# The shared expert's four up blocks, moved from behind the expert sweep into it

## The reference, cut to what matters

```python
def swiglu(x, w1, w3, w2):
    return (jax.nn.silu(x @ w1) * (x @ w3)) @ w2

def moe_ffn(xs, ...):                       # xs: 512 tokens, 64 experts, 6 of them per token
    ...
    yg = lax.map(expert_block, (xg, blk_e)).reshape(P, D) * slot_w[:, None]
    routed = jax.ops.segment_sum(yg, slot_tok, num_segments=T + 1)[:T]
    return routed + swiglu(xs, sh_w1, sh_w3, sh_w2)
```

## Time and profile before

| | us |
|---|---|
| median of 3 runs | 2140.44 (2139.7 to 2141.09) |
| the profiled execution | 2133.77 |
| its span, first to last instruction | 2131.8 |
| PE busy | 1854.0 (87%) |
| DVE busy | 859.0 (40%) |
| ACT busy | 461.1 (22%) |
| POOL busy | 373.6 (18%) |
| transfers, over the span | 625.10 MB, 293 GB/s |

### The profile page before, as it was taken

One profiled execution on the slowest core, in us unless ns is written; L12 is line 12 of the kernel. 1 busy time (PEld: TensorE's weight loads), 2 busy tenths in 40 slices (PEclk: granted clock), 3 DMA queues, 4 the chain that ended last, 5 costly groups with the idle time before them and its releaser, 6 DMA issues.

```text
span 2131.8 us, 30544 instructions
## 1 busy us (share of the span) xinstructions
PE 1854.0 (87%) x9472; PEld 966.6 (45%) x9473; DVE 859.0 (40%) x1527; ACT 461.1 (22%) x823; POOL 373.6 (18%) x563
## 2 busy tenths in 40 slices
PE   5989999885999888788998899876889899989996
PEld 3455555333544444444444443344444444444543
DVE  1546666556322222222115499566222221212226
ACT  4134444212101011111110565220111111101112
POOL 0010000001111111111105288002111111111113
PEclk9999999996999999999999999887999999999997
DMA  9488010347999999999997202256999999999955
GB/s 405 176 340 330 1 40 20 139 173 304 357 420 393 402 400 394 401 404 396 383 382 262 123 1 119 79 227 269 399 406 402 399 387 408 402 400 396 398 182 211
DMA packets 95680, 625.10 MB, mean 293 GB/s; under 512 B 16128, under 2 KB 16256, under 8 KB 57472
## 3 DMA queue, kind: packets, MB, share of 16 engines
q1 hardware_dynamic: 44640, 499.70, 58.3%
q0 software_dynamic: 26112, 79.72, 10.3%
q10 hardware_dynamic: 24864, 44.84, 5.8%
HBM read 563.38 MB, written 76.28 MB: 300 GB/s over the span
## 4 chain that ended last, share of the span: by engine, by line
PE 57%; DMA 19%; DVE 10%; issue 5%; POOL 5%; ACT 3%; SPq 0%; POOLq 0%; DVEq 0%; ACTq 0%
DMA ring<-in 18%; PE PS L1064 12%; PE PS L1058 9%; PE PS L1071 6%; PE PS L1096 4%; PE PS L1085 4%; PE PS L1286 3%; PE PS L1049 3%; PE PS L986 3%; POOL work L581 3%; POOL work L613 3%; PE PS L1040 2%; PE PS L949 2%; PE PS L1004 2%; PE PS L1014 2%
## 5 line engine op out<-in xcount | busy, mean ns | idle before, releaser
L1064 PE MATMUL PS<-ring,work 128*64 128x256 f32 x3360 | 419.6, 406 | 112.8 <-issue 110.2
L1064 PEld LDWEIGHTS PS<-ring,work 128*64 128x64 f32 x3360 | 248.0, 146 | 260.5 <-issue 165.6
L1457 DVE TENSOR_TENSOR work<-work,PS 64x256 f32<-64x256 f32 x105 | 44.4, 423 | 521.9 <-ACT work L666 520.0
L1071 PE MATMUL PS<-ring,work 128*64 128x512 f32 x840 | 203.3, 605 | 1.0 <-DVE work L1469 1.0
L1058 PE MATMUL PS<-ring,work 128*128 128x512 f32 x400 | 184.3, 615 | 19.9 <-issue 8.6
L533 POOL COPY col_i<-idx 128x1 int32 (+1 forms) x128 | 23.4, 182 | 793.2 <-PE PS L1096 785.8
L1463 DVE COPY work<-PS 128x1024 f32<-128x1024 f32 x128 | 156.7, 1225 | 13.6 <-PE PS L1096 9.7
L539 POOL DMA_INDIRECT work<-h_rows,col_i x128 | 124.9, 976 | 165.2 <-issue 165.2
L666 ACT ACTIVATE work<-PS 64x256 f32<-64x256 f32 x105 | 39.5, 376 | 519.1 <-PE PS L1064 516.7
L1096 PE MATMUL PS<-cst,work 128*128 128x128 f32 x1040 | 142.4, 281 | 9.9 <-DMA work<-h_rows,col_i 9.9
L1096 PEld LDWEIGHTS PS<-cst,work 128*128 128x128 f32 x1040 | 115.0, 142 | 62.9 <-issue 52.8
(11 more groups left out here) (247 smaller groups left out, 2176.9 us busy)
## 6 DMA issues: line engine op xcount, KB each, us to landing
ring<-in SPq DMA_DIRECT2D x156, 2048.0 KB, 8.6
ring<-in SPq DMA_DIRECT2D x132, 1024.0 KB, 11.0
y_rows<-sq POOLq DMA_DIRECT2D x2, 14336.0 KB, 58.0
y_rows<-work ACTq DMA_DIRECT2D x210, 128.0 KB
ring<-in SPq DMA_DIRECT2D x3, 4096.0 KB, 15.4
y_rows<-work ACTq DMA_DIRECT2D x46, 256.0 KB
ring<-in SPq DMA_DIRECT2D x2, 3072.0 KB, 16.8
work<-in SPq DMA_DIRECT2D x2, 2048.0 KB, 17.4
```

The source lines that it names most:

```text
L1064: last = mm(bank(6)[64 * q:64 * q + 64, 0:F], lhs(c)[:, 0:64], w13(s)[:, q, c, :], start=(c == 0), stop=(c == DC - 1), tile_position=(0, 6 ...
L1071: last = mm(bank(4)[64 * q:64 * q + 64, :], actT[par][:, kk, 0:64], w2(s)[:, kk, q * 512:(q + 1) * 512], start=(kk == 0), stop=(kk == 1), ...
```

## The change

- SP loads the shared up half (2 MB) into `acc` ahead of the sweep, right behind the fourth expert's weights and ahead of `refill_up(4)`. The load behind the sweep, with its wait, is gone. The down half stays where it was.
- The loops over experts 3 to 62 on TensorE, ACT and DVE are each cut into four loops of 4, 4, 4 and 3 rounds (`PARTS`).
- TensorE runs one shared block behind each of the four: behind experts 18, 34, 50 and 62, that is w1 and w3 for the first half of the features, then for the second half. The third waits for the first silu, the fourth for the first product.
- ACT does the first shared silu and DVE the first shared product behind their second loops. The second silu stays where it was (behind the extra unit); the second product moves ahead of the first combination.
- TensorE behind the sweep: expert 63, the extra unit, then at once the shared down.

```diff
+        shared_w13 = acc.rearrange("p t d -> p (t d)").rearrange("p (a c f) -> p a c f", a=2, c=DC)
+        PARTS = ((0, 4), (4, 8), (8, 12), (12, (E - 4) // 4))
@@ load_moe
+                sp.dma_start(acc.rearrange("p t d -> p (t d)"), sh_w[i][:, 0:UP]).then_inc(sh_in, 16)
                 refill_up(4, slot_of(4))
...
-                sp.wait_ge(m["up_ps"], E - 3)
-                sp.dma_start(slot_ap(SHARED)[:, 0:UP], sh_w[i][:, 0:UP]).then_inc(sh_in, 16)
                 refill_down(E - 1, slot_of(E - 1))
@@ scalar
+                for part, (g0, g1) in enumerate(PARTS):
+                    with nc.scalar.Fori(0, g1 - g0) as g:
...
+                    if part == 1:
+                        shared_silu(0)
...
-                shared_silu(0)
@@ tensor
+                pe.wait_ge(sh_in, 16 + 32 * i)
+                for part, (g0, g1) in enumerate(PARTS):
+                    with nc.tensor.Fori(0, g1 - g0) as g:
+                        for r in range(4):
+                            unit(g * 4 + (4 * g0 + 3 + r), slot_of(3 + r), slot_of(2 + r), g * 32 + (32 * g0 + 32 * loads_of(3 + r)),
+                                 g * 32 + (32 * g0 + 16 * ((4 + r) // 2 + 1)), (1 + r) % 2)
+                    if part == 2:
+                        pe.wait_ge(sh_gate, 1 + 2 * i)
+                    elif part == 3:
+                        pe.wait_ge(sh_act, 1 + 2 * i)
+                    shared_up(part // 2, part % 2)
                 unit(E - 1, slot_of(E - 1), slot_of(E - 2), 32 * loads_of(E - 1), None, 1)
                 either(E - 1, lambda big: down(E - 1, 1, slot_of(E - 1), big))
-                pe.wait_ge(sh_in, 32 * (i + 1))
-                shared_up(0, 0)
...
-                shared_up(0, 1)
-                pe.wait_ge(sh_gate, 1 + 2 * i)
-                shared_up(1, 0)
-                pe.wait_ge(sh_act, 1 + 2 * i)
-                shared_up(1, 1)
+                pe.wait_ge(sh_in, 32 * (i + 1))
                 pe.wait_ge(sh_act, 2 + 2 * i)
@@ vector
+                for part, (g0, g1) in enumerate(PARTS):
...
+                    if part == 1:
+                        shared_product(0)
...
-                shared_product(0)
+                shared_product(1)
                 for n in range(TT * K):
-                    if n == 10:
-                        shared_product(1)
```

More of the change, by code:

```diff
@@ L705, in moe, with shared_silu @@
                 either(1, lambda big: store(1, 0, 1, big))
[L706 to L709, removed]
+                def shared_silu(blk):
+                    a.wait_ge(sh_ps, 2 * blk + 1 + 5 * i)
+                    A(shared[blk], bank(0), ACT.Silu).then_inc(sh_gate, 1)
+                for part, (g0, g1) in enumerate(PARTS):
+                    with nc.scalar.Fori(0, g1 - g0) as g:
+                        for r in range(4):
+                            either(g * 4 + (4 * g0 + 3 + r), lambda big: silu(g * 4 + (4 * g0 + 3 + r), 1, (1 + r) % 2, big))
+                            either(g * 4 + (4 * g0 + 2 + r), lambda big: store(g * 4 + (4 * g0 + 2 + r), g * 64 + (64 * g0 + 32 * (1 + r // 2)),
+                                                                              r % 2, big))
+                    if part == 1:
+                        shared_silu(0)
                 either(E - 1, lambda big: silu(E - 1, 1, 1, big))
@@ L713, in moe @@
                 a.sem_inc(m["t_yev"], 1)
-                def shared_silu(blk):
-                    a.wait_ge(sh_ps, 2 * blk + 1 + 5 * i)
-                    A(shared[blk], bank(0), ACT.Silu).then_inc(sh_gate, 1)
-                shared_silu(0)
                 a.wait_ge(unit_rdy, i + 1)
@@ L1194, in moe, with shared_up @@
                 unit(2, slot_of(2), slot_of(1), 32, 32, 0)
[L1196 to L1199, removed]
+                def shared_up(blk, a):
+                    for c in range(DC):
+                        last = mm(bank(3 * a), shared_w13[:, a, c, blk * 128:blk * 128 + 128], hM[:, c, :], start=(c == 0), stop=(c == DC - 1))
+                    last.then_inc(sh_ps, 1)
+                pe.wait_ge(sh_in, 16 + 32 * i)
+                for part, (g0, g1) in enumerate(PARTS):
+                    with nc.tensor.Fori(0, g1 - g0) as g:
+                        for r in range(4):
+                            unit(g * 4 + (4 * g0 + 3 + r), slot_of(3 + r), slot_of(2 + r), g * 32 + (32 * g0 + 32 * loads_of(3 + r)),
[5 more added lines that the diff above has]
+                    shared_up(part // 2, part % 2)
                 unit(E - 1, slot_of(E - 1), slot_of(E - 2), 32 * loads_of(E - 1), None, 1)
                 either(E - 1, lambda big: down(E - 1, 1, slot_of(E - 1), big))
[L1203 to L1206, removed]
-                pe.wait_ge(sh_in, 32 * (i + 1))
-                shared_up(0, 0)
                 many = nc.tensor.value_load(unit_i[0:1, XMAX:XMAX + 1], min_val=0, max_val=XMAX)
@@ L1605, in moe, with shared_product @@
                 act_out(2, 1, 0)
[L1606 to L1611, removed]
+                def shared_product(blk):
+                    dve.wait_ge(sh_ps, 2 * blk + 2 + 5 * i)
+                    dve.wait_ge(sh_gate, blk + 1 + 2 * i)
+                    V.tensor_tensor(shared[blk], shared[blk], bank(3), ALU.mult).then_inc(sh_act, 1)
+                for part, (g0, g1) in enumerate(PARTS):
+                    with nc.vector.Fori(0, g1 - g0) as g:
+                        for r in range(4):
+                            u = g * 4 + (4 * g0 + 3 + r)
+                            either(u, lambda big: product(u, 1, (1 + r) % 2, big))
+                            rows_out(u + 1, 1, r % 2)
+                            act_out(u, 1, (1 + r) % 2)
+                    if part == 1:
+                        shared_product(0)
                 either(E - 1, lambda big: product(E - 1, 1, 1, big))
```

4 lines of the change are left out of this document (removed).

## The result

The changed kernel takes 2150.17 us in the median of 16 runs, the kernel before 2138.11 us in the median of 16 on the same chip: ratio 1.0056 (95% interval 1.0045 to 1.0067), 12 us slower. The forecast was 2147.9 us, 7.5 us slower, in a range that ends at 2154.5. The profiled executions lie further apart than the medians, 2153.07 us (span 2151.3) against 2133.77 (2131.8); part of it lies in the sweeps, whose length differs by some us from run to run. A second profile of the changed kernel is in the table for that reason.

What follows compares the result with a forecast made beforehand. The weights' DMA pace was taken to bound long stretches of the sweep, TensorE only runs of big experts. Terms -0.8 -1.1 +0.8 +2.4 +4.2 +1.5 +0.5 gave +7.5 us on 2140.44, so 2147.9 us; range 2138.5 to 2154.5.

Steps and rivals of the forecast that it cites:

- Parts 1 and 2: Tail and expert 63: first block leaves the chain, 7.06 us per layer; fourth block lands there, net gain 0.8 and 1.1.
- Part 4: Start of each sweep: the shared up load makes the first token gather late, costing 2.4 us in layer 0, 4.2 in layer 1.
- Rival (a): Start of each sweep: the gather is served in turn, not held up; +0.9 us in all, 2141.3 us; chance 0.22.
- Part 3: Three blocks in each sweep, behind experts 18, 34 and 50: idle time takes up their delay, except 0.8 us in layer 1.
- rival (c): Sweep: blocks are not taken up; blocks 2 and 3 in layer 1 keep 4 us each beyond 0.8; 2155.9 us; chance 0.13.
- the place that the forecast called thin: Third block in layer 1's sweep, behind expert 50: 4.7 us of idle against 7.1, costing 0.8 us.
- Part 2: Fourth block between experts 62 and 63: expert 63 up to 6.2 and 6.0 us later; extra unit's weights still covered.
- Rival (b): Result gathers behind the sweep: issues close up from 1.52 towards 1.24 us, 12.8 us less in all, 2135.1 us; chance 0.10.
- Part 5: Tail: TensorE's clock falls with less work, slowing what follows the last gather; 1.5 us in layer 0, 0.5 behind layer 1.
- signs of being wrong: First up on time; result gathers clearly under 35 us; or a late expert's landing later than the start alone explains.

Runs made afterwards that it cites:

- load_alone: Kernel before plus one unused 2 MB load of the shared up half behind the fourth expert's weights, old load kept; 2143.83 us, ratio 1.0043.
- load_gated: Changed kernel with SP waiting for each layer's first turned rows ahead of the 2 MB shared load; 2141.38 us, ratio 1.0024 to the kernel before.
- again: The changed kernel once more, nothing changed, for a second profile; 2146.77 us, ratio 1.0048 to the kernel before.

## Why the prediction was right, and where its steps were off

**Parts 1 and 2 held.** The first block left the chain and the fourth took its place: -0.9 and -1.3 us against -0.8 and -1.1. The step that left the fourth block on the chain at nearly its full length is confirmed by taking it away: 5.1 and 4.3 us, the rest of the 7.06 going to weights that it had covered. Moving one block that does not come back gives 8 to 9 us.

**Part 4 held in place and nearly in size.** It was named as the dear part, at 6.6 us. To the up of expert 1 it is 2.0 and 6.2 us in the profile, 8.3 together (9.7 in the second profile); the load alone costs 7.5 to 9 us, and gating it gives 5.4 back. In layer 0 the gather takes 7.3 and 8.9 us in the two profiles, where 8.7 was taken. That the profile's 2.0 us come near the 2.4 of the forecast is in part luck: 1.0 is the gather and 1.0 the first up, which ran 6.6 us instead of 5.6, at a granted clock of 0.55. Layer 1's term was too small and lay outside its bound of 4.2: in the six profiles with 16 KB pieces ahead of it the gather takes 9.1 to 9.9 us, where 3.0 + 5.2 = 8.2 was reckoned.

The gather did not come with the end of the queue. By the trace's packets in `load_alone`, the last 16 KB piece of the load starts at 1465.24 and takes 1.29 us; the first gather's last packet follows at 1466.53 and TensorE at 1467.30. In the change it is the same (1470.51, 1.25 us, 1471.76, 1472.73). In both traces the gather was as late as that one piece. The first up then also ran longer at the lower clock, 6.5 us instead of 5.5 (5.9 in the second profile). And the 3.0 us of before are one profile: the other kernels with no load ahead of the gather have 2.7 to 4.7.

**Rival (a) fell, but its rule holds.** It had the gather served in turn and hence not delayed. The runs show both: a delay of 6.7 us in layer 1 with pieces of 16 KB, and of 3.4 with the same bytes in pieces of 4 KB, and in both the gather's packets run while pieces of the load still do. Service in turn does not mean an equal share, when the other queue's turns are four times as long. The Trainium skill, "DMA: Bandwidth & Descriptors" (Queues, rings and completion order), has an engine change queues only between packets; the two runs agree with it, and the result that rival (a) drew from it, no cost, is what was wrong. That rule does not give the 2.6 us more that pass before the gather's first packet, with either size.

**Part 3 failed.** It took +0.8 us for three blocks in each sweep, on the ground that the transfers don't pause for a late TensorE. They do: the refills wait for the up and down that the block delays, and SP issues them in order. The rows above show the share at 0.41 and 0.54 at 1803 to 1809 us, and in layer 0 it dips likewise behind the second block (0.58 in 850 to 855). The dip comes again in the second profile (0.46 in 1803 to 1806) and in `load_gated` (0.53 in 1795 to 1800). In size, from windows over whole sweeps (up of expert 1 to up of expert 62): the four kernels without a block in the sweep have 554.3 to 558.7 us in layer 0, mean 555.9, and 552.4 to 555.6 in layer 1, mean 553.9; the seven with three blocks in this stretch have 558.2 to 560.7, mean 559.3, and 555.2 to 560.2, mean 557.8. That is 3.5 and 3.9 us, 7.3 together before rounding, instead of 0.8 (bounds 0 and 2.4). After:

```profile
534.10:1094.80 560.70, 505.92 (x2981) 264.36 (x2981) 134.57 (x213) 64.27 (x123) 82.36 (x185) 0.97 0.99 389
1486.60:2046.80 560.20, 517.52 (x2934) 269.51 (x2934) 133.79 (x212) 64.63 (x123) 82.66 (x185) 0.98 0.99 392
```

Before it is a share of 1.00 at 394 GB/s and 1.01 at 399. The idle time of the earlier trace rows was there; what the forecast missed is that a late TensorE also shifts the refills that wait for it. This is rival (c)'s outcome, at half its price in layer 1 (3.9 us, where 0.8 + 8 were reckoned), and the same again in layer 0, which (c) left out.

Most of it is the second block's. The lag of an up against the kernel before, counted from the up of expert 1, worked out from timeline rows ("gated" is `load_gated`, which has the same three blocks):

```
                        layer 0                  layer 1
up of expert       after  again  gated      after  again  gated
18                  +1.1   +1.8   -0.5       -0.8   -1.2   -1.3
34                  +1.9   +1.9   +0.5       +1.6   -1.6   +0.6
35                  +8.6  +10.3   +7.1       +8.5   +5.3   +7.5
50                  +4.2   +5.5   +3.3       +6.3   +2.3   +5.0
62                  +5.2   +4.8   +4.1       +6.6   +1.7   +4.0
```

From expert 34 to 50 the second block leaves 2.3 to 3.6 us in layer 0 and 3.9 to 4.7 in layer 1; `load_alone`, with no block there, differs from before by -0.1 and +1.1. The first leaves -0.4 to 2.4 and the third -1.0 to 1.0. So the place that the forecast called thin was free, the second in layer 1, which it gave nothing with 7.0 us of idle time as the reason, was the dearest, and the second in layer 0 it did not price at all, nor the first in layer 1. Moving that block changed the profile and not the time.

**Missed: the extra unit's store.** The forecast had everything between the extra unit and the gathers alike. The first block had hidden the wait for expert 62's store beside 6 MB of weights; without it layer 0 is 3.4 and 3.6 us longer there, half of it ACT's wait and half the slower down behind it. Part 2 had asked who covers the extra unit's weights and not who covers ACT's wait.

**Rival (b) came in part.** The result gathers' issues span 33.6 us in layer 0 and 32.6 in layer 1, where it was 34.9 and 35.9; to the turned sums 1.9 and 2.5 us are won. But the load alone, with all blocks in the tail, also shows 1.0 and 2.7 us there, so they are not clearly the blocks'. They did not close up to 1.24 us each, as the rival had it; the DMA share of 0.93 there fits the reason that the prediction gave against it.

**Part 5 held in size.** From the turned sums on, layer 0 is 1.8 us longer in one profile and 0.8 in the other (forecast 1.5), layer 1 0.3 (forecast 0.5). The window over the gathers says 0.74 (0.73 up to 1185) where "near 0.5" was expected, against 0.90 in the earlier trace rows; TensorE is busy 24 of 35 us there, partly because it is slow:

```profile
1140.00:1175.00 35.00, 24.32 (x77) 15.11 (x78) 24.64 (x22) 0.00 (x0) 26.31 (x24) 0.74 0.93 336
```

The estimate behind it, 0.2 us for each sum of squares, does not follow from a factor of two on 0.43 us, which is 0.43 more; the one slow sum of the earlier trace rows, 0.65 us, shows 0.22.

**The signs.** In layer 0 experts 24 and 40 stand on landings of their weights again, and expert 63 starts 6.9 us after expert 62's last matmul, as forecast. Two of the signs of being wrong came as well: the result gathers take less than 35 us (33.6 and 32.6), and the queue did run thin behind the second block.

**The sum.** Parts 2 and 5 as forecast, part 4 +1.7, part 3 +6.5, the store +3.4, the tails -4.4: 7.5 + 7.2 = 14.7 us, against 10.4 to 12 measured by medians; the 3 to 4 us between them are open. The sign and the dear part were right. That the total came close is in part luck: costs of 11.6 us were missing, and 4.4 us of gain, and the loss is still 10.4 to 12 us where 7.5 were forecast.

## What to carry to other kernels

Move only the work that is on the chain: three of these four blocks were nearly free where they stood, and bringing their 2 MB forward cost 7.5 to 9 us, about what the one block gives when it leaves the chain for good (8 to 9). Before a bulk load is put ahead of a small gather that everything waits for, gate it on the gather's arrival, or cut it into pieces of the gather's size. In a ring whose refills wait for the consumer, slack at the consumer is also slack in the queue; and when a block leaves, list every wait of every engine that it had covered.

## What the runs showed of the hardware that was not expected

- The piece size of a neighbouring queue changes a gather's delay: 2.7 to 4.7 us with a queue that is running empty, 9.6 beside 16 KB pieces, 6.4 beside the same bytes in 4 KB pieces (layer 1).
- Beside a full queue the gather's first packet runs 4.1 to 4.2 us after the issue, with either piece size, and 1.6 us after it beside a queue that is running empty. Why is open.
- With 16 KB pieces the gather's last packet waited for one late piece (1465.24, 1.29 us long) while most engines were idle (share 0.56 in 1464 to 1466). Why that piece came so late is open.
- A pair of stores of 128 KB beside 6 MB of loads took 12.7 us (the median of such stores is 9.3), while the same 6 MB beside result gathers stretched 24 of them from 35.5 to 49.0 us.
- An idle wait of 2 to 4 us ahead of a big up cost TensorE twice: the up behind it took 8.8 to 10.0 us at a granted clock of 0.81 to 0.71, where it takes 7.1 at 1.00.
